# Split products for eleven of the mixer's twelve q, k and recurrence projections

## What is computed

```python
h = rmsnorm(x, mix_norm[l])
z = h @ w_in[l]
q, k, v, f_logit, gate_in, rec_in = jnp.split(z, split_points, axis=-1)
log_f = jax.nn.log_sigmoid(f_logit + b_forget[l])
att = forgetting_attention(q, k, v, log_f)      # 8 heads of 64, decay = differences of cumsum(log_f)
rec = causal_depthwise_conv(rec_in, conv_w[l], conv_b[l])
rec = rg_lru(rec, w_a[l], b_a[l], w_x[l], b_x[l], lru_lambda[l])
lru_out = rec * jax.nn.gelu(gate_in, approximate=True)
x = x + jnp.concatenate([att, lru_out], axis=-1) @ w_out[l]
```

## Time and profile before

| | |
|---|---|
| median of three executions | 1412.73 us (1411.54 to 1414.36) |
| the profiled execution, own time | 1413.81 us |
| its span in the profile | 1412.0 us |
| TensorE busy | 1323.9 us, 94% of the span |
| VectorE busy | 630.1 us, 45% |
| ScalarE busy | 527.0 us, 37% |
| mean granted TensorE clock | 0.976 |
| read from memory | 236.59 MB |

### The profile page before, as it was taken

The page is one execution under the profiler, slowest core; times in us unless marked ns, Lnnn a source line. Parts: engine busy times, 40 slices in busy tenths (PEclk is TensorE's granted clock), DMA queues, the critical chain, the costliest instruction groups (busy, mean ns, idle before and its releaser), DMA issues. The chain is left out here.

```text
span 1412.0 us, 19330 instructions
## 1 busy us (share of the span) xinstructions
PE 1323.9 (94%) x7954; PEld 1005.2 (71%) x7954; DVE 630.1 (45%) x1093; ACT 527.0 (37%) x885; POOL 67.2 (5%) x92
## 2 busy tenths in 40 slices
PE   5999989899999999999989889999999989999996
PEld 2777666676788888878866679998676566666663
DVE  2323564566233343478346875667413152222212
ACT  2356334444723232325563566443234121111112
POOL 0000002231000000011000230000000000000000
PEclk7999989999999999999999999999999999999998
DMA  9522120327122252224331103563331859999980
GB/s 386 195 82 90 64 116 31 149 91 269 60 90 90 94 203 91 90 98 146 126 117 60 61 31 135 191 216 145 108 119 60 357 201 380 397 415 403 419 362 32
DMA packets 34222, 238.97 MB, mean 169 GB/s; under 512 B 4304, under 2 KB 4432, under 8 KB 6224
## 3 DMA queue, kind: packets, MB, share of 16 engines
q1 hardware_dynamic: 34128, 237.66, 43.7%
HBM read 236.59 MB, written 1.05 MB: 168 GB/s over the span
## 5 line engine op out<-in xcount | busy, mean ns | idle before, releaser
L229 DVE TENSOR_TENSOR pieces_lo<-weight_ring,pieces_hi 128x1024 fp32r<-128x1024 f32 x154 | 187.7, 1223 | 283.0 <-ACT pieces_hi L221 282.7
L247 PE MATMUL proj<-h_hi,pieces_hi 128*128 128x512 f32 (+1 forms) x816 | 290.3, 356 | 5.9 <-DVE h_lo L1145 2.9
L248 PE MATMUL proj<-h_lo,pieces_hi 128*128 128x512 f32 (+1 forms) x816 | 284.9, 349 | 0.0
L249 PE MATMUL proj<-h_hi,pieces_lo 128*128 128x512 f32 (+1 forms) x816 | 283.4, 347 | 0.0
L221 ACT ACTIVATE pieces_hi<-weight_ring 128x1024 fp32r<-128x1024 f32 x158 | 165.3, 1053 | 95.9 <-PE score L249 50.7
L247 PEld LDWEIGHTS proj<-h_hi,pieces_hi 128*128 128x128 f32 x816 | 156.1, 191 | 36.8 <-issue 10.1
L248 PEld LDWEIGHTS proj<-h_lo,pieces_hi 128*128 128x128 f32 x816 | 156.3, 192 | 21.7 <-issue 2.0
L249 PEld LDWEIGHTS proj<-h_hi,pieces_lo 128*128 128x128 f32 x816 | 156.1, 191 | 20.2
L1943 PE MATMUL turn<-expert_parts,e_gathered 128*64 128x256 f32 x768 | 85.3, 379 | 0.8 <-DVE e_gathered L2132 0.8
L1943 PEld LDWEIGHTS turn<-expert_parts,e_gathered 128*64 128x64 f32 x768 | 55.9, 137 | 32.4 <-issue 7.3
L1078 ACT ACTIVATE l_merge_gate<-proj 128x512 f32<-128x512 f32 (+1 forms) x48 | 23.5, 490 | 125.4 <-PE proj L249 125.4
(11 more groups left out here) (440 smaller groups left out, 2033.8 us busy)
## 6 DMA issues: line engine op xcount, KB each, us to landing
weight_ring<-in_stream SPq DMA_DIRECT2D x110, 1024.0 KB, 4.8
expert_parts<-in_experts SPq DMA_DIRECT2D x70, 1024.0 KB, 11.0
weight_ring<-in_experts SPq DMA_DIRECT2D x26, 1024.0 KB, 11.0
l_rows<-in_rows SPq DMA_DIRECT2D x2, 768.0 KB, 15.6
l_y_attn<-in_ada_first SPq DMA_DIRECT2D x1, 1024.0 KB, 5.2
l_y_gla<-in_ada_first SPq DMA_DIRECT2D x1, 1024.0 KB, 7.3
l_y_sgu<-in_ada_first SPq DMA_DIRECT2D x1, 1024.0 KB, 8.2
l_q<-in_ada_first SPq DMA_DIRECT2D x1, 1024.0 KB, 10.1
```

The source lines that it names most:

```text
L229: eng.tensor_tensor(self.part(self.lo_ring[:, n % NPIECE, :], kind), self.raw(slot, c, kind), self.part(self.hi_ring[:, n % NPIECE, :], ki ...
L247: pe.matmul(out, sh, mh, start=start, stop=False)
L248: pe.matmul(out, sh, ml, start=False, stop=False)
L249: return pe.matmul(out, sl, mh, start=False, stop=stop)
```

## The change

All rec, q and k pieces but rec 0 become split products. The mixer's input `hT` is split once, into `XH` and `XL`; each piece of weights is split into a ring of three places, `WH` and `WL`. These four tensors, 40 KB per partition, lie where `CAT`, `PR`, `PTB`, `CB`, `RG`, `IG` and `V` lie, which are written only later. The weights' layout in memory changes so that a piece is 1024 consecutive values per partition, and half of a name's weights is freed when its two pieces are done. The list of steps changes: f stands behind rec 0, cum behind k, and the exponentials and logarithms of f and lambda are taken in pairs (`fexp`, `fln`).

```diff
+SPLIT, SPLIT_RING = ("rec", "q", "k"), 3
+SPLIT_PIECES = [(n, i) for n in SPLIT for i in range(4)][1:]
+
 def mixer_schedule():
     steps = [("norm", t) for t in range(2)] + [("turnx", i) for i in range(4)]
-    steps += [("rec", i) for i in range(4)] + [("f", 0)] + [("q", i) for i in range(4)] + [("cum", 0)]
-    steps += [("lambda", 0)] + [("k", i) for i in range(4)] + [("ri", i) for i in range(4)]
-    steps += [("v", 0), ("lru", 0), ("v", 1)]
+    steps[2:2] = [("whi", p) for p in SPLIT_PIECES[:SPLIT_RING]]
+    steps += [("xsplit", i) for i in range(4)] + [("wlo", SPLIT_PIECES[0]), ("wlo", SPLIT_PIECES[1])]
+    steps += [("rec", 0), ("f", 0)]
+    for n, piece in enumerate(SPLIT_PIECES):
+        if n + 2 < len(SPLIT_PIECES):
+            steps += [("wlo", SPLIT_PIECES[n + 2])]
+        steps += [piece]
+        if n + SPLIT_RING < len(SPLIT_PIECES):
+            steps += [("whi", SPLIT_PIECES[n + SPLIT_RING])]
+        steps += {("rec", 2): [("fexp", 0)], ("rec", 3): [("fln", 0)], ("q", 0): [("fsum", 0), ("lambda", 0)]}.get(piece, [])
+    steps += [("cum", 0)] + [("ri", i) for i in range(4)] + [("v", 0), ("lru", 0), ("v", 1)]
...
+        with ExitStack() as early:
+            XH, XL = (early.enter_context(nc.sbuf_tensor(f"x_in_{n}", [P, KT, T], F32R)) for n in ("hi", "lo"))
+            WH, WL = (early.enter_context(nc.sbuf_tensor(f"x_weights_{n}", [P, SPLIT_RING, KT, P], F32R)) for n in ("hi", "lo"))
+        CAT = sb("mixed", [P, 8, T])
+        PR, PTB = sb("probs", [P, 2, 2, T]), sb("probs_t", [P, 2, 2, T])
+        CB = sb("cum_decay_rows", [P, 3, 8, P])
+        RG, IG = sb("r_gate", [P, 4, T]), sb("i_gate", [P, 4, T])
+        V = sb("v", [P, 2, 512])
...
+                elif (kind, i) in SPLIT_PIECES:
+                    n = SPLIT_PIECES.index((kind, i))
+                    acc = PJ.open(pe, J(kind, i))
+                    pe.wait_ge(*sig.min_lo.at(4))
+                    pe.wait_ge(*sig.w_lo.at(n + 1))
+                    wh, wl = WH[:, n % SPLIT_RING], WL[:, n % SPLIT_RING]
+                    for k in range(KT):
+                        last = split_product(pe, acc[:, 0:T], (wh[:, k], wl[:, k]), (XH[:, k, :], XL[:, k, :]), k == 0, k == KT - 1)
+                    last.then_inc(*PJ.done())
+                    W.last_read(f"x.{kind}", PJ.ready(J(kind, i)), (i // 2,))
...
+                elif kind == "fexp":
+                    link(act.activation(lam[:, 0:4], par[:, M_LAM:M_LAM + 4], ACT.Abs))
                     act.wait_ge(*PT.ready(J("f")))
                     link(act.activation(FT[:], PT.tile(J("f"))[0:8, 0:T], ACT.Abs, bias=par[0:8, M_BF:M_BF + 1]))
+                    link(act.activation(lam[:, 0:4], lam[:, 0:4], ACT.Exp, scale=-1.0))
                     link(act.activation(FT[:], FT[:], ACT.Exp, scale=-1.0))
+                elif kind == "fln":
+                    act.activation(lam[:, 0:4], lam[:, 0:4], ACT.Ln, bias=one).then_inc(*sig.lam.one())
                     act.activation(FT[:], FT[:], ACT.Ln, bias=one[0:8]).then_inc(*sig.fsoft.one())
+                elif kind == "whi":
+                    n = SPLIT_PIECES.index(i)
+                    act.wait_ge(*W.has_landed(f"x.{i[0]}", i[1] // 2))
+                    if n >= SPLIT_RING:
+                        act.wait_ge(*PJ.ready(J(*SPLIT_PIECES[n - SPLIT_RING])))
+                    act.activation(WH[:, n % SPLIT_RING], raw(*i), ACT.Copy).then_inc(*sig.w_hi.one())
+                elif kind == "xsplit":
+                    act.wait_ge(*PJ.evacuated(J("turnx", i)))
+                    act.activation(XH[:, 2 * i:2 * i + 2, :], hT[:, 2 * i:2 * i + 2, :], ACT.Copy)\
+                        .then_inc(*sig.min_hi.one())
...
+                elif kind == "xsplit":
+                    dve.wait_ge(*sig.min_hi.at(i + 1))
+                    k = slice(2 * i, 2 * i + 2)
+                    dve.tensor_tensor(XL[:, k, :], hT[:, k, :], XH[:, k, :].bitcast(F32), ALU.subtract)\
+                        .then_inc(*sig.min_lo.one())
+                elif kind == "wlo":
+                    n = SPLIT_PIECES.index(i)
+                    dve.wait_ge(*sig.w_hi.at(n + 1))
+                    dve.tensor_tensor(WL[:, n % SPLIT_RING], raw(*i), WH[:, n % SPLIT_RING].bitcast(F32), ALU.subtract).then_inc(*sig.w_lo.one())
```

More of the change, by code:

```diff
@@ L315, in __init__ @@
         self.lru_seq = signal("lru_seq")
+        self.min_hi = signal("mixer_in_hi")
+        self.min_lo = signal("mixer_in_lo")
+        self.w_hi = signal("w_hi")
+        self.w_lo = signal("w_lo")
         self.gelu = signal("gelu")
@@ L1454, in mixer @@
         FT = sb("f_tmp", [8, T])
-        CB = sb("cum_decay_rows", [P, 3, 8, P])
         inverse = sb("inverse_sums", [P, 4, 2])
-        PR, PTB = sb("probs", [P, 2, 2, T]), sb("probs_t", [P, 2, 2, T])
         small = sb("small", [P, 2, 8])
@@ L1460, in mixer, with raw @@
         lam = sb("lambda", [P, 16])
+        with ExitStack() as early:
[6 more added lines that the diff above has]
+        V = sb("v", [P, 2, 512])
+        def raw(kind, i):
+            return W.half(f"x.{kind}", i // 2)[:, i % 2 * PIECE:(i % 2 + 1) * PIECE].rearrange("p (k c) -> p k c", c=P)
         block = ctx.enter_context(nc.Block())
@@ L1496, in _ @@
                     last.then_inc(*PT.done())
-                elif kind in ("rec", "q", "k", "gat"):
-                    w = slot(kind)
+                elif (kind, i) in SPLIT_PIECES:
[8 more added lines that the diff above has]
+                    W.last_read(f"x.{kind}", PJ.ready(J(kind, i)), (i // 2,))
+                elif kind in ("rec", "gat"):
+                    if kind == "rec":
+                        pe.wait_ge(*W.has_landed("x.rec", 0))
+                        w = raw("rec", 0)
+                    else:
+                        w = slot(kind)
                     acc = PJ.open(pe, J(kind, i))
@@ L1505, in _ @@
                     last.then_inc(*PJ.done())
-                    used(kind, PJ.ready(J(kind, i)))
+                    if kind == "gat":
+                        used(kind, PJ.ready(J(kind, i)))
                 elif kind == "v":
@@ L1596, in _ @@
                     act.activation(st[:, 4 + i:5 + i], st[:, i:i + 1], ACT.Sqrt, bias=eps).then_inc(*sig.norm_root.one())
-                elif kind == "lambda":
-                    x = par[:, M_LAM:M_LAM + 4]
-                    link(act.activation(lam[:, 0:4], x, ACT.Abs))
-                    link(act.activation(lam[:, 0:4], lam[:, 0:4], ACT.Exp, scale=-1.0))
-                    act.activation(lam[:, 0:4], lam[:, 0:4], ACT.Ln, bias=one).then_inc(*sig.lam.one())
-                elif kind == "f":
+                elif kind == "fexp":
+                    link(act.activation(lam[:, 0:4], par[:, M_LAM:M_LAM + 4], ACT.Abs))
                     act.wait_ge(*PT.ready(J("f")))
                     link(act.activation(FT[:], PT.tile(J("f"))[0:8, 0:T], ACT.Abs, bias=par[0:8, M_BF:M_BF + 1]))
+                    link(act.activation(lam[:, 0:4], lam[:, 0:4], ACT.Exp, scale=-1.0))
                     link(act.activation(FT[:], FT[:], ACT.Exp, scale=-1.0))
+                elif kind == "fln":
+                    act.activation(lam[:, 0:4], lam[:, 0:4], ACT.Ln, bias=one).then_inc(*sig.lam.one())
                     act.activation(FT[:], FT[:], ACT.Ln, bias=one[0:8]).then_inc(*sig.fsoft.one())
+                elif kind == "whi":
[8 more added lines that the diff above has]
+                        .then_inc(*sig.min_hi.one())
                 elif kind in ("rec", "q", "k", "v"):
@@ L1679, in _ @@
                     dve.tensor_scalar(lam[:, 8:12], lam[:, 12:16], 8.0, None, ALU.mult).then_inc(*sig.lam.one())
-                elif kind == "f":
+                elif kind == "xsplit":
[7 more added lines that the diff above has]
+                    dve.tensor_tensor(WL[:, n % SPLIT_RING], raw(*i), WH[:, n % SPLIT_RING].bitcast(F32), ALU.subtract).then_inc(*sig.w_lo.one())
+                elif kind == "fsum":
                     dve.wait_ge(*sig.fsoft.at(1))
@@ L2357, in layouts @@
     for n, a in (("q", 0), ("k", 512), ("v", 1024), ("gat", 1544), ("rec", 2056)):
-        put(f"x.{n}", w[:, a:a + 512])
+        put(f"x.{n}", w[:, a:a + 512], "cols" if n in SPLIT else "rows")
     for n in range(2):
```

3 lines of the change are left out of this document (removed).

## The result

| | before | after |
|---|---|---|
| median | 1411.67 us (1411.44 to 1414.36, 6 runs) | 1406.14 us (1402.89 to 1407.11, 6 runs) |
| ratio of the two, 95% interval | | 0.995 [0.9936, 0.9964] |
| profiled execution, own time | 1413.81 us | 1403.08 us |
| its span | 1412.0 us | 1401.2 us |
| its mean granted clock | 0.976 | 0.984 |

The change makes the kernel faster by 0.5%, 5.5 us between the medians; forecast were 1405.9 us and 6.8 us of gain. The profiled execution of the changed kernel is one of its two fastest, and its clock is one of the two highest of its six: the two with a clock of 0.984 took 1403.08 and 1402.89, the three with 0.975 to 0.978 took 1406.99 to 1407.11. So this trace shows more than the change typically gives, and its 10.8 us of difference in span have to be taken apart.

The account below looks back on a forecast made before the run. TensorE was taken as the bound, busy 1323.9 of 1412.0 us. Rec to v falls from 56.13 to 48.07 us, gain 8.06, less 1.3 for the clock: 6.8 us, so 1405.9 us from the median of 1412.73; range 1403.4 to 1409.2.

Parts of the forecast that it names:

- The price of a piece: Rec, q and k on TensorE: a split piece costs 2.88 us, as in the trunk; a plain rec piece 3.48.
- The rival of cheaper pieces: Split products in half the plain spacing, 0.109 us: a piece 2.61, gain 3.0 us larger, 1402.9 us; chance 0.03.
- the one of exposed weight loads: Weight loads of 0.19 us in the open: 4.56 us a split piece, 11.9 us lost, 1424.6 us; chance 0.04.
- the rule that it set against the row: Skill page's issue gap, N/2.4 + 2.5 ns: 109 ns at 256 columns, 2.62 us a split piece, sum larger by 2.9 us.
- f as cover: Start of rec: rec 0 and f keep TensorE busy until 1005.0, so nothing of the first splits is in the open.
- The supply: Split operands from ScalarE and VectorE come in time, except q 3's low part: TensorE waits 0.3 us there.
- The rival in which the supply binds: Table loads and convolutions hold up splits by 1 us each for four pieces: gain about 3, 1409.7 us; chance 0.07.
- Cum and ri: Both now stand together behind k and keep their old times on TensorE, 4.38 and 4.68 us.
- Nothing added: Ri needs the banks cum just filled, but its wait there falls together with its wait for ScalarE's 1.28 us table load.
- The clock: One lower-clock stretch over ri and the start of v, about 1.3 us lost, ends 0 and 3.2; chance 0.48.
- the rival that was called two stretches: Ri and v both at the lower clock, or one in the attention: gain 4.9 us, 1407.8 us; chance 0.11.
- Nothing is given back behind v: From v to the end: no transfer holds TensorE, so a microsecond won before v is one at the end.

Follow-up runs that it names:

- the plain order: The changed kernel's step list, weight layout and release by halves, but all twelve pieces plain float32 products without splitting; 1412.44 us against 1413.22, ratio 0.9995.
- second trace: The changed kernel measured and profiled once more with nothing altered, on another occasion; 1408.04 us against 1412.52, ratio 0.9967.

## Why the prediction was right, point by point

**The price of a piece: right.** 2.88 was taken from the trunk, 2.90 came over eleven pieces, and the plain order gave 3.47: 11 x 0.57 = 6.3 us, the body of the gain. The rival of cheaper pieces (2.61, from half of the plain spacing) falls, and so does the one of exposed weight loads. Two slips in the prediction's reasoning did no harm. The 512-column records of the earlier trace rows start 0.23 us apart and not 0.24; over eight of them there (978.91 to 980.78) it is 0.234, so that its lower bound is 2.8 and not 2.9, a little under the 2.88 that it took. And by the rule that it set against the row, the sum would be smaller by 2.9 us, not larger; the forecast did not use that rule.

**f as cover: right.** No wait with it, one of 1.4 us without it.

**The supply: right in kind, 0.3 us of wait too many.** At q 2 the low part, begun at 1013.98, is ready at 1015.2, 1.0 us ahead; q 3's, the first of the pair at 1017.18, is ready at 1018.4, some 0.7 ahead where the prediction had it 0.2 late. VectorE had the forget gate's sum and lambda done in 1017.18 - 1015.11 = 2.1 us instead of 2.3, and began them sooner. The wait of 0.3 us did not come in either trace of the changed kernel. The rival in which the supply binds did not come true, but the kernel with doubled low parts shows how it looks: 4.9 us of waits, gain zero.

**Cum and ri: the sum right, the parts not.** "Nothing added" was said of the banks that both use. At full clock (cum over 128 rows) they take 8.87 us, against 4.38 + 4.68 = 9.06 in the sum, 0.2 less: ri now waits 0.49 for the bank, but its wait for the gates, 0.99 before, is down to 0.26. The two waits did fall together.

**The clock: the step that was mis-sized.** Without a fall the changed kernel takes 47.74 us from rec to v (48.07 in the prediction's sum). It lost 1.3 us to the clock in the prediction, "a little less than 1.6 because some of ri waits anyway". In the first trace it lost 49.18 - 47.74 = 1.4. But in the second it lost 50.28 - 47.74 = 2.5, and cum and ri, 8.87 at full clock, took 11.26 to 11.63 in the three other kernels that keep a whole cum of eight rows ahead of ri. So in four traces of five the price is 2.4 to 2.8 us: near the rival that was called two stretches (3.2 us lost), given 0.11. What stood there was one stretch about twice as long: the granted clock was low for about 3.5 us in the first trace and for about 7 in the second (1038.8 to 1045.7). At 1.2 GHz eight records of cum take 3.78 instead of 1.99 us (plain order). Behind cum there now stand more short groups with waits between them than the k pieces were. That these make the stretch longer is only argued; that it mostly costs more than the 1.3 of the forecast is measured. The prediction also took the earlier trace rows for the place of the one fall; the same trace has another at the experts' start (0.72, above), which it left out of account.

**What the medians say.** A typical gain is then 56.13 - (47.74 + 2.5) = 5.9 us, and the two medians give 5.5 and 4.5 us; the rest, 0.4 to 1.4 us, is within what the fall at the experts' start moves: in the second trace rec to v is 5.85 us shorter than before and v to the end 1.59 longer, 4.3 in all. How often that fall comes in executions that were not profiled is not known. The forecast of 1405.9 is met by a median of 1406.14, and that is in part luck: the median before was itself 1.1 us lower in this measurement than the one the forecast was made from, and the gain was 5.5 us where 6.8 had been forecast.

**Nothing is given back behind v: right, as far as waits go.** From v to the end it is 357.43 us in the first trace and 359.45 in the second, against 357.86; both differences go with the clock at the experts' start, and no new wait stands there. k's first half is asked for at 1004.86 instead of 1012.02, about 3 us before the forecast, as rec started 3.4 earlier; no wait for a transfer came of either. Table loads on ScalarE in the mixer are down by two (L1639 and L1642 stand once each where before there were two of either kind).

## What to carry to other kernels

Read the price of a product from another place in the same kernel where the same form already runs, and check only whether its operands come in time: that gave 2.88 against 2.90. Where a short group of products that fill few of the array's rows stands among long ones, look at the granted clock behind it in several traces, and try zero-filled rows, which cost no time on TensorE. One profiled execution says little about what the clock costs; the same code gave 1.4 and 2.5 us between rec and v, and nothing and 2.0 us behind v.
